# Convolution of a decoder block: 13 tap pairs on TensorE and five taps on VectorE, with three weight remainders made by GpSimd

## The reference, cut to what matters

```python
attn = _sliding_window_attention(q, k, v, sinks[i])
conv = _conformer_conv(ca, cg, conv_w[i], conv_b[i], conv_ln_g[i], conv_ln_b[i])
mixed = jnp.concatenate([_rms_norm(attn, attn_out_norm[i]),
                         _rms_norm(conv, conv_out_norm[i])], axis=-1)
h = h + mixed @ w_out[i]

def _conformer_conv(a, g, w_dw, b_dw, ln_g, ln_b):
    u = a * jax.nn.sigmoid(g)
    y = lax.conv_general_dilated(u, w_dw[:, None, :].astype(u.dtype), window_strides=(1,),
        padding=[(CONV_WIDTH - 1, 0)], dimension_numbers=('NWC', 'WIO', 'NWC'),
        feature_group_count=CONV_CH) + b_dw
    return jax.nn.silu(_layer_norm(y, ln_g, ln_b))
```

## Time and profile before

| | before |
|---|---|
| median of three runs | 1392.18 us (1391.82 to 1392.21) |
| profiled execution, its own time | 1391.11 us |
| span of the profiled execution | 1389.3 us |
| mean granted TensorE clock, of full speed | 0.999 |
| busy: TensorE matmul / weight load | 1379.0 / 1163.3 us |
| busy: VectorE / ScalarE / GpSimd | 968.7 / 830.2 / 25.5 us |
| HBM, mean over the span | 179 GB/s |

### The profile page before, as it was taken

The page is one execution under the profiler, slowest core; times in us unless marked ns, Lnnn a source line. Parts: engine busy times, 40 slices in busy tenths (PEclk is TensorE's granted clock), DMA queues, the critical chain, the costliest instruction groups (busy, mean ns, idle before and its releaser), DMA issues.

```text
span 1389.3 us, 21669 instructions
## 1 busy us (share of the span) xinstructions
PE 1379.0 (99%) x8083; PEld 1163.3 (84%) x8083; DVE 968.7 (70%) x1399; ACT 830.2 (60%) x1274; POOL 25.5 (2%) x37
## 2 busy tenths in 40 slices
PE   9999999999999999999999999999999999999997
PEld 7777788888888888887888888888888878888886
DVE  5878866775657777577876675676675678777756
ACT  7689746554356554468865554565554688655544
POOL 2100000000000000000000000000000000000000
PEclk9999999999999999999999999999999999999999
DMA  8933565656566665543566665566665434666650
GB/s 290 343 94 106 172 191 173 193 189 198 191 188 198 189 188 199 162 146 101 176 197 191 191 211 191 168 184 193 190 199 158 152 107 156 205 185 189 213 188 31
DMA packets 130157, 249.62 MB, mean 180 GB/s; under 512 B 8552, under 2 KB 12992, under 8 KB 130080
## 3 DMA queue, kind: packets, MB, share of 16 engines
q1 hardware_dynamic: 127680, 240.58, 55.4%
q0 software_dynamic: 2240, 7.73, 1.7%
q10 hardware_dynamic: 160, 0.27, 0.1%
HBM read 247.49 MB, written 1.05 MB: 179 GB/s over the span
## 4 chain that ended last, share of the span: by engine, by line
PE 99%; ACT 0%; DVE 0%; issue 0%; POOL 0%; ACTq 0%; DVEq 0%; POOLq 0%
PE acc L2399 16%; PE acc L2401 16%; PE acc L2400 16%; PE acc L2765 14%; PE pair L2765 7%; PE acc L2771 7%; PE turns L2765 6%; PE pair L2771 4%; PE turns L2771 3%; PE turns L2412 3%; PE pair L2887 2%; PE pair L2437 1%; PE turns L2458 1%; PE acc L2484 1%; PE turns L2553 0%; PE pair L2534 0%
## 5 line engine op out<-in xcount | busy, mean ns | idle before, releaser
L1429 DVE TENSOR_TENSOR w_lo<-stage,w_hi 128x1024 fp32r<-128x1024 f32 (+2 forms) x462 | 551.1, 1202 | 294.1 <-ACT w_hi L773 288.9
L773 ACT ACTIVATE w_hi<-stage 128x1024 fp32r<-128x1024 f32 (+2 forms) x462 | 475.3, 1040 | 403.2 <-PE acc L2401 191.8
L2765 PE MATMUL acc<-x,w_hi 128*128 128x512 f32 x832 | 229.1, 393 | 0.0
L2765 PEld LDWEIGHTS acc<-x,w_hi 128*128 128x128 f32 x832 | 149.3, 189 | 26.1 <-DVE x L1483 0.8
L2399 PE MATMUL acc<-w_hi,x_hi 128*128 128x512 f32 (+2 forms) x432 | 170.3, 394 | 0.0
L2401 PE MATMUL acc<-w_hi,x_lo 128*128 128x512 f32 (+2 forms) x432 | 163.8, 379 | 0.0
L2400 PE MATMUL acc<-w_lo,x_hi 128*128 128x512 f32 (+2 forms) x432 | 163.7, 379 | 0.0
L2399 PE MATMUL acc<-w_hi,g_hi 128*128 128x512 f32 x352 | 137.3, 390 | 0.0
L2400 PE MATMUL acc<-w_lo,g_hi 128*128 128x512 f32 x352 | 137.0, 389 | 0.0
L2401 PE MATMUL acc<-w_hi,g_lo 128*128 128x512 f32 x352 | 137.0, 389 | 0.0
L2771 PE MATMUL acc<-x,w_lo 128*128 128x256 f32 x832 | 136.2, 282 | 0.0
(11 more groups left out here) (399 smaller groups left out, 1784.3 us busy)
## 6 DMA issues: line engine op xcount, KB each, us to landing
stage<-in_ffn_w_gate_up SPq DMA_DIRECT2D x176, 512.0 KB, 3.8
stage<-in_ffn_w_down SPq DMA_DIRECT2D x88, 512.0 KB, 4.4
stage<-in_w_ff SPq DMA_DIRECT2D x64, 512.0 KB, 4.1
stage<-in_w_in SPq DMA_DIRECT2D x62, 512.0 KB, 4.4
stage<-in_w_out SPq DMA_DIRECT2D x16, 512.0 KB, 3.9
stage<-in_w_ple_gate SPq DMA_DIRECT2D x16, 512.0 KB, 4.5
stage<-in_w_lru_up SPq DMA_DIRECT2D x8, 512.0 KB, 3.9
stage<-in_w_o SPq DMA_DIRECT2D x8, 512.0 KB, 4.3
```

What stands on the lines that cost most here:

```text
L773: act.activation(w_hi[:, n.slot(SPLIT), 0:t, 0:w], stage[:, n.slot(STAGE), 0:t, 0:w], ACT.Copy).then_inc(hi_done, 1)
L1429: dve.tensor_tensor(w_lo[:, n.slot(SPLIT), 0:t, 0:w], stage[:, n.slot(STAGE), 0:t, 0:w], w_hi[:, n.slot(SPLIT), 0:t, 0:w].bitcast(F32), AL ...
L2765: pe.matmul(banks[m], w_hi[:, n.slot(SPLIT), q, m * P:(m + 1) * P], x2[:, kt, :], start=kt == 0, stop=False)
```

## The change

The number of tap pairs on TensorE falls from 14 to 13, so `LATE` grows from 3 to 5, with it `taps_late` and the loop in `late_taps`. On VectorE both halves of the copies now stand ahead of both halves of the late taps. The remainders of units 0 and 1 of Lout_a0 and of unit 0 of Lout_a1 are made by GpSimd (`rest_of_unit`): it waits for `hi_done` of the unit, subtracts, and counts `s_pool_lo`. VectorE no longer makes these three; in the places shown it waits for `s_pool_lo` and for the count of `lo_done` so far, and raises `lo_done` itself (`rest_by_pool`), so that the units still count in their order.

```diff
--- before.py
+++ after.py
@@ -65,7 +65,7 @@
 PHI_PART = P // QUAD
 PHI_ROUNDS = 2 * KPHI // PHI_PART
 TAP_PAIRS = (TAPS2 + 1) // 2
-PAIRS_PE = 14
+PAIRS_PE = 13
 ACT_BLOCKS = (2, 3)
 LATE = TAPS2 - 2 * PAIRS_PE
 WINDOW = 128
@@ -449,6 +449,7 @@
         landed = [sem(f"landed{i}") for i in range(STAGE)]
         hi_done = sem("hi_done")
         lo_done = sem("lo_done")
+        s_pool_lo = sem("s_pool_lo")
         unit_used = sem("unit_used")
         acc_free = [sem(f"acc_free{i}") for i in range(2)]
         turn_done = sem("turn_done")
@@ -734,6 +735,13 @@
             wait(pool, s_h, RESIDUAL.at("d", 3))
             p_rows = a["p_2"].rearrange("l o (t p) n -> p (l o t) n", p=P)
             for layer in range(layers):
+                def rest_of_unit(name, i):
+
+                    n = UNITS.at(name, i, layer)
+                    wait(pool, hi_done, n + 1)
+                    pool.tensor_tensor(w_lo[:, n.slot(SPLIT), :, :], stage[:, n.slot(STAGE), :, :],
+                                       w_hi[:, n.slot(SPLIT), :, :].bitcast(F32), ALU.subtract).then_inc(s_pool_lo, 1)
+
                 if layer:
                     wait(pool, turn_hi, HI_TURNS.at("Lp", 1, layer - 1))
                 pool.dma_start(pcur[:, :, :], p_rows[:, layer * TT:(layer + 1) * TT, :]).then_inc(s_pcur, 16)
@@ -743,12 +751,15 @@
                 else:
                     pool.wait_ge(s_emb, layer)
                 pool.dma_start(gn[:, :], a["ple_norm_2"][layer].partition_broadcast(P)).then_inc(s_late, 16)
+                for i in range(2):
+                    rest_of_unit("Lout_a0", i)
                 pool.wait_ge(s_sqattn, layer + 1)
                 pool.tensor_tensor(att_sums[:, 0:2 * S], att_sq[:, 0:2 * S], att_sq[:, 2 * S:4 * S],
                                    ALU.add).then_inc(s_att_sums, 1)
                 pool.wait_ge(s_att_sums, 2 * layer + 1)
                 pool.tensor_tensor(att_sums[:, 2 * S:3 * S], att_sums[:, 0:S], att_sums[:, S:2 * S],
                                    ALU.add).then_inc(s_att_sums, 1)
+                rest_of_unit("Lout_a1", 0)
                 wait(pool, s_ysq, Count(4, [(layer, 4)]))
                 pool.tensor_tensor(att_sums[:, 0:2 * S].rearrange("p (n s) -> p n s", s=S), ysq[:, 0:2, :], ysq[:, 2:4, :],
                                    ALU.add).then_inc(s_conv_sums, 1)
@@ -2192,14 +2203,20 @@
                     wait(dve, s_late_taps, Count(half + 1, [(layer, 2)]))
                     dve.sem_inc(turn_free[TURNS.at("Lu", half, layer).slot(2)], 1)
 
+                def rest_by_pool(name, i, count):
+
+                    wait(dve, s_pool_lo, Count(count, [(layer, 3)]))
+                    wait(dve, lo_done, UNITS.at(name, i, layer))
+                    dve.sem_inc(lo_done, 1)
+
                 for half in range(2):
                     shifted_half(half)
-                    if half == 1:
-                        split("Lout_a0", layer, units=[0])
+                for half in range(2):
                     wait(dve, s_shifted, Count(half + 1, [(layer, 2)]))
                     wait(dve, s_in_place, Count(half + 1, [(layer, 2)]))
                     late_taps(half)
-                split("Lout_a0", layer, units=[1])
+                for i in range(2):
+                    rest_by_pool("Lout_a0", i, i + 1)
                 for k in range(2):
                     wait(dve, s_mixhi, Count(k + 1, [(layer, 2)]))
                     for p in (2 * k, 2 * k + 1):
@@ -2207,7 +2224,6 @@
                         ins = dve.scalar_tensor_tensor(x_lo[:, p, :], mixt2[:, p, :], vec2[:, layer, at:at + 1],
                                                        x_hi[:, p, :].bitcast(F32), ALU.mult, ALU.subtract)
                     ins.then_inc(s_mixlo, 1)
-                split("Lout_a1", layer, units=range(1))
                 wait(dve, s_conv, Count(1, [(layer, 1)]))
                 for k in range(2):
                     of = slice(2 * k, 2 * k + 2)
@@ -2227,6 +2243,7 @@
                 wait(dve, s_yin, Count(2, [(layer, 2)]))
                 summed = note(dve.tensor_tensor(group_sums[:, :, :], y[:, 0:2, :], y[:, 2:4, :], ALU.add))
                 sum_halves(summed)
+                rest_by_pool("Lout_a1", 0, 3)
                 split("Lout_a1", layer, units=range(1, 2))
                 at = STATS["attn"]
                 wait(dve, s_rattn, Count(1, [(layer, 1)]))
```

## The result

The changed kernel takes 1400.27 us (median of 6 runs, 1399.25 to 1401.68); the kernel before, on the same chip, takes 1392.45 us (6 runs, 1391.82 to 1393.09). The ratio is 1.0056, 95% interval 1.0045 to 1.0067: slower by 0.56%, 7.8 us. Slower was forecast, and TensorE waits as forecast, but the predicted 1396.8 us holds little more than half of the loss and the range ended at 1398.0.

A forecast was written before the change was run, and what follows sets the result against it. TensorE, busy 1379.0 of 1389.3 us, was taken as the bound. A late x_lo costs it 2.31 us a layer despite the shorter convolution: 1392.18 + 4.6 = 1396.8 us, with an 8-in-10 range of 1391.8 to 1398.0.

The forecast's parts named there:

- The convolution: TensorE: 26 instead of 28 pair rounds a layer end it 0.875 us earlier, 1.75 us for two layers.
- The late taps: VectorE: four instead of two pairs of L2187 a half, 4.64 us each; half 1 ends at 659.06 us.
- The waits of the queue: VectorE ahead of x_lo: 0.14 us of existing queue work plus 0.14 us for the new waits and increments.
- rival B: VectorE starts first, all four x_lo pass ahead of GpSimd's third unit; 0.3 us lost, 1392.5 us; chance 0.17.
- Rival C: Nobody is held, since the holding shown is of TENSOR_TENSOR, not L2207's kind; 2 x 0.07 us, 1392.3 us; chance 0.11.
- GpSimd's unit: GpSimd's remainder of 1024 columns takes 2.42 us, bounds 2.24 to 2.96; the third runs 659.30 to 661.72 us.
- rival E: GpSimd needs more than 2.42 us for an fp32r output of 1024 columns; 1399.0 us with 3.5 us; chance 0.05.
- The holding: VectorE's x_lo, with two SBUF inputs, is held until GpSimd's third unit ends at 661.72 us; TensorE restarts at 663.30.
- D: x_lo is in time after all; up to the full gain of 1.75 us, 1390.4 us; chance 0.07.
- 2.31 us lost a layer, 4.6 us in all: TensorE restarts after the convolution at 663.30 instead of 660.99 us, waiting for x_lo; the loss counted for two layers.
- Behind that nothing new is late: After x_lo, sums for L2953 end about 665.8, before TensorE arrives at 666.6 us; no further loss.

The follow-up runs named there:

- experiment 2: Changed kernel with only the third GpSimd remainder (unit 0 of Lout_a1) back on VectorE, behind the sums for L2953: 1393.57 us, ratio 1.0007.
- experiment 3: Changed kernel with GpSimd's third unit made to wait for x_lo: 1393.49 us, ratio 1.0009.
- experiment 6: Changed kernel with GpSimd raising lo_done itself and VectorE's waits and increments for the three units gone, but one wait: 1400.91 us, ratio 1.0061.
- experiment 1: Changed kernel with 7 rounds of 8 further matmuls on TensorE between the convolution's end and the wait for x_lo: 1396.59 us, ratio 1.003.
- experiment 7: Changed kernel with the four x_lo moved ahead, behind the second pair of half 1's late taps: 1391.58 us, ratio 0.9993.
- experiment 4: Kernel before with PAIRS_PE = 13 and nothing else, no remainder on GpSimd: 1399.60 us, ratio 1.0057.

## Why the prediction was wrong

Measured from the start of the convolution, 648.74 us before and 649.37 after, its steps compare as follows.

**The convolution** ends 0.86 us earlier in layer 0, against 0.875 forecast: 416 instructions in 11.46 us instead of 448 in 12.32. In layer 1 it took 11.64 us; x_lo was later still, so this cost nothing.

**The late taps**: forecast to start at 0.90 and to end at 10.32 us; they start at 0.90 and end at 10.36. The sum of pairs and gaps was right.

**The waits of the queue** ahead of x_lo: 0.28 us in the forecast, 0.43 measured. x_lo started at 10.79 instead of 10.60. This changed nothing in the changed kernel, where GpSimd decides. In experiment 2, with x_lo unheld, the 0.19 us are most of what lies between the 0.32 us measured there and the 0.07 of rivals B and C.

**GpSimd's unit**: forecast 2.42 us, starting at 10.56; measured 2.36, starting at 10.58. The line through 256 and 512 columns held, also with the fp32r output (rival E is out).

**The holding**: forecast to bring the last x_lo at 14.50 us and TensorE at 14.56; measured 14.40 and 14.51. Experiments 2 and 3 confirm the cause by taking the overlap away, and experiment 6 shows that GpSimd gets in behind the first of the four even when VectorE is first, so rival B is out. Rival C is out by the 2.43 us of the first x_lo, and D since TensorE waited 3.05 us.

**The step that failed** is "2.31 us lost a layer, 4.6 us in all": it priced a wait of TensorE at its length. I read the clock at 1.00 in both stretches and carried that level over to a kernel in which TensorE stands still for 3 us; the longest wait in the trace of before is 1.17 us, at 5.7 us. "Behind that nothing new is late" looked only for late engines. The wait itself was right (2.26 us measured). The missing term is 1.58 us a layer in the profiled run, 3.2 us in all, and experiment 1 gives it independently: 7.8 - 4.4 = 3.4 us. The Trainium skill, TensorE: Matmul & The Clock Gate, "Part 1: The HAM clock gate", says that the clock returns to the lower level when TensorE has been idle and needs activity to rise again; the trace agrees (0.51 of full speed behind 3.05 us without a matmul), and it should have been a rival with a price. A bound was in the trace of before: the matmuls of Lout_a0 start 0.23 us apart at 1.00, and at half the clock at most twice that, an estimate; 0.42 was measured. So the 3.28 us of work behind the wait could cost up to 3.3 us more.

The range was too narrow for the same reason. It took in GpSimd's duration and the start times to a tenth of a microsecond and held TensorE's own speed for certain.

## What to carry to other kernels

Where one engine is busy 99% of the time, first ask of a change what must be ready at the moment that its shortened work ends; here the convolution ended 0.875 us a layer earlier, and x_lo, even unheld (experiment 2), came 1.1 us too late for that. A wait of TensorE of about 3 us cost its length and, in the 3.28 us of work behind it, between nothing and 2.8 us of clock, so bound it with both levels. Work given to GpSimd was free here beside VectorE operations with at most one SBUF input; look in the timeline for the places where it meets one with two, on both sides: which engine is held, and who waits for that one. Moving the operation that TensorE waits for (experiment 7) gave back the whole loss of 7.8 us, though no more.

## What the runs showed of the hardware

- The fall of the clock is not the same each time. Behind 2.9 to 3.05 us without matmuls the stretch that takes 3.28 us at full clock took 4.86 twice (the changed kernel), 6.11 and 4.83 (experiment 6), and 3.48 at a clock of 1.00 and 6.08 at 0.50 (experiment 4). Behind 0.9 to 1.1 us it did not fall in any of the four profiled layers of experiments 2 and 3.
- Nor does it come at a fixed place. In both layers of the changed kernel the first matmuls behind the wait ran at full pace for about 1 us, and the slow ones followed, although TensorE was busy again. In layer 1 of experiment 4 and layer 0 of experiment 6 the clock was at 0.50 from the first matmul behind the wait.
- VectorE and GpSimd hold each other by the single operation, whichever is first: 0.48 us of VectorE lengthened GpSimd's by 0.2 us, and GpSimd's 2.4 us lengthened VectorE's next from 0.48 to 2.57 us (experiment 6). Where they start within 0.02 us of each other, either can be held: VectorE's remainder for 0.58 us in fourteen profiled layers, GpSimd's sum for 1.07 us in six.
- Behind the late taps VectorE stood idle for 0.43 us with two times two waits and an increment in its queue beside what stands there anyway (changed kernel), and for 0.15 us without them (experiment 6, 659.01 to 659.16).
